# A two-block transformer in fp32r on one core: latent heads in pairs, convolution taps by a table, split weights in halves, other banks, output units among the odd attention's last steps

## What is computed

```python
def even_mixer(h, w_in, q_norm_a, k_norm_a, q_lora_norm, kv_lora_norm, w_uq, w_uk, w_uv, w_out, ...):
    qa, ka, va, ga, cq, ckv, kr, gb = jnp.split(h @ w_in, splits, axis=-1)
    ...
    oa = dense_gqa_attention(qa, ka, va) * jax.nn.silu(ga)
    cq, ckv = rms_norm_2(cq, q_lora_norm), rms_norm_2(ckv, kv_lora_norm)
    qb = (cq @ w_uq).reshape(b, s, B_HEADS, B_NOPE + B_ROPE)
    q_nope, q_rope = qb[..., :B_NOPE], qb[..., B_NOPE:]
    q_rope, k_rope = apply_rope(q_rope, ...), apply_rope(kr, ...)
    q_lat = jnp.einsum('bshd,chd->bshc', q_nope, w_uk)
    ob = mla_attention(q_lat, q_rope, ckv, k_rope, w_uv) * jax.nn.silu(gb)
    return jnp.concatenate([oa, ob], axis=-1) @ w_out

def odd_mixer(h, w_in, sink, w_out, slopes):
    qc, kc, vc, gc = jnp.split(h @ w_in, ...)
    oc = windowed_sink_attention(qc, kc, vc, sink, slopes)      # 16 heads, window 128
    return (oc * jax.nn.silu(gc)) @ w_out
```

## Time and profile before

| | |
|---|---|
| median of 3 executions | 1345.56 us |
| lowest, highest | 1342.73, 1348.53 us |
| profiled execution, its own time | 1347.7 us |
| span of its trace | 1345.9 us |
| TensorE matmul busy | 1308.7 us, 97% |
| VectorE busy | 824.9 us, 61% |
| ScalarE busy | 441.8 us, 33% |
| GpSimd busy | 682.8 us, 51% |
| mean granted TensorE clock | 0.986 |

### The profile page before, as it was taken

The page is one execution under the profiler, slowest core; times in us unless marked ns, Lnnn a source line. Parts: engine busy times, 40 slices in busy tenths (PEclk is TensorE's granted clock), DMA queues, the critical chain, the costliest instruction groups (busy, mean ns, idle before and its releaser), DMA issues.

```text
span 1345.9 us, 19639 instructions
## 1 busy us (share of the span) xinstructions
PE 1308.7 (97%) x7126; PEld 1031.0 (77%) x7126; DVE 824.9 (61%) x1586; ACT 441.8 (33%) x943; POOL 682.8 (51%) x627
## 2 busy tenths in 40 slices
PE   7999999999999999999999999999999999999996
PEld 5898776788888888888888888877566888866575
DVE  4798689933554777777775258654775354055633
ACT  5201455523111212221111243245766223145511
POOL 5864222235676666666677555643000285656650
PEclk9999899999999999999999989999999999999997
DMA  5622101112353455555553224211000122311111
GB/s 178 237 74 78 32 33 33 32 61 81 94 172 96 170 188 190 198 199 195 188 188 101 71 85 142 79 63 48 1 1 1 63 84 84 100 36 48 32 48 63
DMA packets 37524, 130.22 MB, mean 97 GB/s; under 512 B 4544, under 2 KB 4928, under 8 KB 37184
## 3 DMA queue, kind: packets, MB, share of 16 engines
q1 hardware_dynamic: 26640, 93.07, 21.9%
q10 hardware_dynamic: 10800, 35.98, 7.2%
HBM read 126.94 MB, written 2.10 MB: 96 GB/s over the span
## 4 chain that ended last, share of the span: by engine, by line
issue 46%; POOL 36%; PE 16%; DVE 1%; POOLq 1%; ACT 0%; DVEq 0%; ACTq 0%
POOL wlo L1054 21%; PE bank L467 12%; POOL whi L1051 12%; POOL whi L1050 3%; PE bank L980 1%; PE bank L1010 1%; PE bank L990 1%; POOLq L1053 0%; DVE arena L2350 0%; PE bank L538 0%; DVE xbuf L2154 0%; POOL arena L1088 0%; PE bank L555 0%; PE bank L484 0%; POOL wlo L1079 0%
## 5 line engine op out<-in xcount | busy, mean ns | idle before, releaser
L1054 POOL TENSOR_TENSOR wlo<-raw,whi 128x1024 fp32r<-128x1024 f32 x163 | 400.4, 2456 | 13.6
L1050 POOL TENSOR_TENSOR whi<-raw,ones 128x2 fp32r<-128x2 f32 x163 | 42.9, 263 | 571.5 <-DMA raw<-in_w 571.3
L467 PE MATMUL bank<-ysplit,whi 128*128 128x512 f32 x984 | 313.3, 397 | 0.9 <-POOL wlo L1054 0.9
L467 PE MATMUL bank<-hhi,whi 128*128 128x512 f32 x536 | 219.4, 409 | 0.4 <-DVE arena L2217 0.4
L467 PEld LDWEIGHTS bank<-ysplit,whi 128*128 128x128 f32 x984 | 183.6, 189 | 37.6 <-POOL wlo L1054 1.3
L467 PE MATMUL bank<-hhi,wlo 128*128 128x512 f32 x536 | 210.9, 393 | 0.0
L467 PE MATMUL bank<-hlo,whi 128*128 128x512 f32 x536 | 210.5, 393 | 0.0
L467 PE MATMUL bank<-ysplit,wlo 128*128 128x512 f32 x496 | 194.2, 392 | 0.0
L1051 POOL TENSOR_SCALAR whi<-raw 128x1022 fp32r<-128x1022 f32 x163 | 178.1, 1092 | 0.0
L467 PEld LDWEIGHTS bank<-hhi,whi 128*128 128x128 f32 x536 | 101.6, 189 | 25.7 <-issue 6.6
L467 PEld LDWEIGHTS bank<-hhi,wlo 128*128 128x128 f32 x536 | 101.6, 190 | 22.4
(11 more groups left out here) (313 smaller groups left out, 2183.4 us busy)
## 6 DMA issues: line engine op xcount, KB each, us to landing
raw<-in_w SPq DMA_DIRECT2D x171, 512.0 KB, 3.6
arena<-in_ada ACTq DMA_DIRECT2D x48, 512.0 KB, 4.3
xbuf<-in_xT ACTq DMA_DIRECT2D x12, 256.0 KB, 5.3
xbuf<-in_w ACTq DMA_DIRECT2D x1, 2048.0 KB, 10.1
first<-in_w ACTq DMA_DIRECT2D x1, 2048.0 KB, 8.6
out_t<-xbuf SPq DMA_DIRECT2D x8, 256.0 KB, 2.1
xbuf<-in_xT SPq DMA_DIRECT2D x4, 256.0 KB, 6.6
first<-in_uq ACTq DMA_DIRECT2D x1, 768.0 KB, 8.3
```

The costliest lines, as they stand in the source:

```text
L467: m = mm(b[:, :], w[:, s, k * P:(k + 1) * P], x, start=(k == 0 and part == 0), stop=(k == DC - 1 and part == 2))
L1050: g.tensor_tensor(whi[:, s, 0:2], raw[:, s, 0:2], ones[:, :], ALU.mult)
L1054: g.tensor_tensor(wlo[:, s, :], raw[:, s, :], whi[:, s, :].bitcast(F32), ALU.subtract)\
```

## The change

What it does, part by part:

1. **Taps by a table.** `TAPS_AT` gives the number of taps after each step of N: 21 instead of 12 in steps 0 to 11, 50 instead of 66 in steps 12 to 31, 4 in steps 32 and 33, and 3 behind the loop's step 34.
2. **The compressed softmax in PSUM.** `cmp_max` adds, takes the maximum and subtracts in the score bank, and only the last product goes to SBUF. The bank is given back after it.
3. **Low parts in halves.** `low_half` replaces the one 128x1024 operation by two of 128x512.
4. **Biases.** The third bias of e and of o goes to bank 4 (`BIAS_BANK`), and no longer waits for bank 3.
5. **Banks.** `O_BANKS` is (3, 0, 1, 2), equal to `E_BANKS` and `EOUT_REST` and so on their turn; `oq` 3 takes its bank from it and no longer from `TR`. `ekr` takes its bank from `E_BANKS`. `C_FILL` is (3, 0).
6. **Three units' high parts on ScalarE** (`ACT_HIGH`, the last three output units of e).
7. **Latent heads in pairs.** The 64 unrotated rows of two heads make one 128-row product: 4 `key_prep` and 4 `query_prep`, and the rotated rows of four heads one more, twice (`PREP_R`). The rotation of the key moves to steps 1 and 2. All are split in high and low parts (ScalarE `prep_high`, VectorE `prep_low`), and the scores are 3 pairs of 64-row and 3 pairs of 32-row matmuls in fp32r.
8. **The odd attention's end.** `OOUT_FIRST` puts 21 pieces (63 matmuls) of the first three output units in steps 28 to 35, into banks 0, 3 and 7.
9. **The last norm.** The spread is made twice, in two banks. ScalarE copies the second to SBUF, and GpSimd does 3 of the 8 products (`Z_POOL`), for which ScalarE has applied the gain ahead. The stores go in the order `Z_STORE`.

```diff
-PREP_V = (12, 13, 14, 15)
-PREP_K = {12: 0, 13: 1, 14: 2, 15: 3, 20: 4, 21: 5, 24: 6, 25: 7}
-PREP_Q = {12: 0, 13: 1, 16: 2, 17: 3, 20: 4, 21: 5, 24: 6, 25: 7}
+PREP_V = (15, 16, 17, 18)
+PREP_K = {12: 0, 13: 1, 20: 2, 24: 3}
+PREP_Q = {11: 0, 13: 1, 21: 2, 25: 3}
+PREP_R = {10: 0, 19: 1}
+KEY_ROPE = 1
-TAPS_LIGHT = 12
+OOUT_FIRST = {28: ((0, 0, 2),), 29: ((0, 2, 4),), 30: ((0, 4, 6),), 31: ((1, 0, 3),), 32: ((1, 3, 6),), 33: ((2, 0, 3),),
+              34: ((2, 3, 6), (0, 6, 7)), 35: ((1, 6, 7), (2, 6, 7))}
+OOUT_BANKS, OOUT_REST = (0, 3, 7), (1, 2, 0, 3)
+Z_POOL = (0, 1, 2)
+TAPS_AT = (1, 1, 1, 1, 4, 1, 3, 1, 2, 1, 3, 2, 3, 3, 3, 2, 3, 2, 3, 1, 3, 2, 3, 2, 3, 3, 3, 1, 3, 2, 3, 2, 2, 2)
...
-RAW_BANKS, BIAS_BANK = (0, 1, 2), (3,)
+RAW_BANKS, BIAS_BANK = (0, 1, 2), ((3,), (4,))
-O_BANKS = (3, 0, 1, 2, 3, 0, 1, 2)
+O_BANKS = (3, 0, 1, 2)
+ACT_HIGH = (("eout", 5), ("eout", 6), ("eout", 7))
...
-                    for half in range(2):
-                        x = p % 2 * 2 + half
-                        m = mm(banks[half][:, :], QF[x][0:96, qt * P:(qt + 1) * P], KF[x][0:96, :], start=True, stop=True)
+                    j = p - 4
+                    for part, (x, y) in enumerate(((0, 0), (1, 0), (0, 1))):
+                        for half in range(2):
+                            rows = slice(64 * half, 64 * half + 64)
+                            mm(banks[half][:, :], QN[j % 2][x][rows, qt * P:(qt + 1) * P], KN[j % 2][y][rows, :],
+                               start=(part == 0), stop=False)
+                    for part, (x, y) in enumerate(((0, 0), (1, 0), (0, 1))):
+                        for half in range(2):
+                            rows = slice(64 * half + 32 * (j % 2), 64 * half + 32 * (j % 2) + 32)
+                            m = mm(banks[half][:, :], QR[j // 2][x][rows, qt * P:(qt + 1) * P], KR[y][rows, :],
+                                   start=False, stop=(part == 2))
...
-            def key_prep(h):
-                b = bank.take(pe, AB_FILL_BANK if h in (2, 3) else C_R, ("KF", h))
-                mm(b[0:64, :], uk[:, h * HD:(h + 1) * HD], eckv[:, :], start=True, stop=True)\
-                    .then_inc(*pe_did.up(("KF", h)))
+            def key_prep(j):
+                b = bank.take(pe, C_R, ("KN", j))
+                mm(b[:, :], uk[:, j * P:(j + 1) * P], eckv[:, :], start=True, stop=True).then_inc(*pe_did.up(("KN", j)))
...
                 unit("oq", i, first=(lambda k: dve_did.at(("o", "h", k))) if i == len(RAW_O) else None,
-                     pool=TR if i == len(RAW_O) else O_BANKS)
+                     pool=O_BANKS)
...
+                for j, k0, k1 in OOUT_FIRST.get(i, ()):
+                    if k0 == 0:
+                        oout[j] = unit("oout", j, src=y_parts, first=lambda k: dve_did.at(("oy", k)), inline=False,
+                                       pool=OOUT_BANKS)
+                    for k in range(k0, k1):
+                        oout[j](k)
...
+            def low_half(s, half):
+
+                at = slice(half * D // 2, (half + 1) * D // 2)
+                return g.tensor_tensor(wlo[:, s, at], raw[:, s, at], whi[:, s, at].bitcast(F32), ALU.subtract)
...
-                g.tensor_tensor(wlo[:, s, :], raw[:, s, :], whi[:, s, :].bitcast(F32), ALU.subtract)\
-                    .then_inc(w_split.sem, 1)
+                low_half(s, 0)
+                low_half(s, 1).then_inc(w_split.sem, 1)
...
+            pool.wait_ge(*act_did.at(("z", "rsb")))
+            for c in Z_POOL:
+                g.tensor_tensor(xT[:, c, :], xT[:, c, :], rsb, ALU.mult).then_inc(*pool_did.up(("res", c)))
...
-                link(V.tensor_tensor(c3, c3, nmax[:, x:x + 8].unsqueeze(2).to_broadcast([P, HEADS, NCP]), ALU.subtract))
-                V.tensor_tensor(c3, c3, col("slope8", 0, HEADS).unsqueeze(2).to_broadcast([P, HEADS, NCP]), ALU.mult)\
+                link(V.tensor_tensor(S, S, nmax[:, x:x + 8].unsqueeze(2).to_broadcast([P, HEADS, NCP]), ALU.subtract))
...
+                V.tensor_tensor(c3, S, col("slope8", 0, HEADS).unsqueeze(2).to_broadcast([P, HEADS, NCP]), ALU.mult)\
...
-                if i < n:
-                    taps(1 if i < TAPS_LIGHT else -(-len(steps) // (n - i)))
+                if i <= len(TAPS_AT):
+                    taps(TAPS_AT[i] if i < len(TAPS_AT) else len(steps))
```

More of the change, by code:

```diff
@@ L480, in bias @@
                 if k == 0:
-                    bank.take(pe, BIAS_BANK, (tag, "bias", j))
-                b = bank.tiles[BIAS_BANK[0]]
+                    bank.take(pe, BIAS_BANK[j // 2], (tag, "bias", j))
+                b = bank.tiles[BIAS_BANK[j // 2][0]]
                 for w in (whi, wlo):
@@ L548, in sums_once, with spread @@
                     m.then_inc(*pe_did.up((name, "sum")))
-            def spread(name, c0, pool=TR, at=0):
+            def spread(name, c0, pool=TR, at=0, key="spread"):
                 pe.wait_ge(*dve_did.at((name, "stat")))
-                b = bank.take(pe, pool, (name, "spread"))
+                b = bank.take(pe, pool, (name, key))
                 for tt in range(TT):
@@ L556, in spread @@
                            ident[:, :], start=True, stop=True)
-                m.then_inc(*pe_did.up((name, "spread")))
+                m.then_inc(*pe_did.up((name, key)))
             def norm(name, c0=0):
@@ L828, in _ @@
             raw_units("e", 0, RAW_E, raw_e, double_sums, lambda: spread("e", 0, at=TT))
-            unit("ekr", 0, first=lambda k: dve_did.at(("e", "h", k)), pool=TR)
+            unit("ekr", 0, first=lambda k: dve_did.at(("e", "h", k)), pool=E_BANKS)
             spread("f", 0)
@@ L1028, in _ @@
                     c_values(i - 3)
-            for i in range(DC):
-                unit("oout", i, src=y_parts, first=(lambda k: dve_did.at(("oy", k))) if i == 0 else None)
+                for j, k0, k1 in OOUT_FIRST.get(i, ()):
[4 more added lines that the diff above has]
+                        oout[j](k)
+            for j in range(len(oout)):
+                oout[j](DC - 1)
+            for i in range(len(oout), DC):
+                unit("oout", i, src=y_parts, pool=OOUT_REST)
             sums_once("z")
             spread("z", 0)
+            spread("z", 0, key="spread2")
         @block.gpsimd
@@ L1076, in split_part @@
                     return
[L1077 removed]
                 pool.wait_ge(w_hi.sem, u + 1)
[L1079 removed]
+                m = low_half(s, part - 1)
                 if part == 2:
@@ L1095, in c_sink @@
                     .then_inc(*pool_did.up(("C", "sink", i)))
+            splits(0, UNIT[ACT_HIGH[0]])
+            for unit_ in ACT_HIGH:
+                u = UNIT[unit_]
+                pool.wait_ge(w_hi.sem, u + 1)
+                low_half(u % WS, 0)
+                low_half(u % WS, 1).then_inc(w_split.sem, 1)
             end = UNIT[("og", 0)] + WS
-            splits(0, end)
+            splits(UNIT[ACT_HIGH[-1]] + 1, end)
             pool.wait_ge(*dve_did.at("nsink"))
@@ L1603, in _ @@
                 square("z", i, xT[:, i, :], dve_did.at(("x4", i)))
+                if i in Z_POOL:
+                    act.wait_ge(*sq_ready.at(("z", i)))
+                    A(xT[:, i, :], xT[:, i, :], ACT.Copy, scale=col("fn", i)).then_inc(*act_did.up(("z", "gain", i)))
             root("z")
+            act.wait_ge(*pe_did.at(("z", "spread2")))
+            A(rsb, bank.of(("z", "spread2"))[:, :], ACT.Copy).then_inc(*act_did.up(("z", "rsb")))
         @block.vector
@@ L2152, in norm_in_place @@
                 dve.wait_ge(*pe_did.at((name, "spread")))
-                for c in range(DC):
+                for c in range(len(Z_POOL), DC):
                     V.scalar_tensor_tensor(xT[:, c, :], xT[:, c, :], gain(c), bank.of((name, "spread"))[:, :],
@@ L2249, in ab_max, with rope_part, prep_low @@
                         .then_inc(*sm_ready.up(("AB", s)))
[L2251 to L2261 removed]
+            def rope_part(x, part, key):
+                if part == 0:
+                    link(V.stream_shuffle(ropet, x, [(j + 16) % 32 for j in range(32)]))
+                    link(V.tensor_tensor(ropet, ropet, sinT, ALU.mult))
+                else:
+                    link(V.tensor_tensor(x, x, cosT, ALU.mult))
+                    V.tensor_tensor(x, x, ropet, ALU.add).then_inc(*dve_did.up(key))
+            def prep_low(name, j, to):
+                dve.wait_ge(*act_did.at((name, j)))
+                V.tensor_tensor(to[j % 2][1], bank.of((name, j))[:, :], to[j % 2][0].bitcast(F32), ALU.subtract)\
+                    .then_inc(*dve_did.up((name, j)))
+                bank.freed((name, j), dve_did, (name, j))
             def ab_out(p):
@@ L2507 @@
     cosT, sinT = np.cos(angT), np.sin(angT) * sign
+    uq = a["b_w_uq_2"][0].reshape(2, P, HEADS, 96)
+    rope_heads = [[4 * j + 2 * (g % 2) + g // 2 for g in range(4)] for j in range(2)]
+    uq = np.stack([uq[:, :, 2 * j:2 * j + 2, 0:HD].reshape(2, P, P) for j in range(4)]
```

(1 more changed line is left out.)

112 lines of the change are left out of this document (73 added, 39 removed).

## The result

The changed kernel takes 1349.88 us (median of 20 executions, 1342.86 to 1351.12), the kernel before 1345.55 (20 executions in the same rounds). The ratio is 1.0034, 95% interval 1.0019 to 1.0048: slower by a third of a percent, where 1333 and a gain of 0.9% were forecast. Both had a granted clock of 0.986, where 14 of the 20 executions of the changed kernel had 0.984 or less; so the two spans are equal, although the medians differ by 4.3 us.

The account below looks back on a forecast made before the run. TensorE, its matmuls busy 97% of the span, was taken as the bound. The terms summed to −13.8 us: 1333.9 from the profiled 1347.7, 1331.8 against the median; 1333 was given, range 1322 to 1341.

Parts of the forecast that it names:

- Third bias: Bias matmuls of e and o: two waits of 1.1 us go, as bank 4 has nothing to wait for; −0.8.
- `oq` 3: In o, TensorE waits for `oq` 2's bank, +5.0 us; a possible clock fall behind it, bounds 0 and 5.1, +2.5.
- N and the fall at 147: In N, five waits on VectorE's maxima go, −5.9 us, and the half-clock stretch behind 147 us goes, −4.9.
- the allowance of 1.0: In N, 1.0 us of the 6.9 of waits was allowed to stay or come anew.
- both causes go: In N, the SBUF subtraction beside GpSimd (1.87 us wait) and the late taps (5.0 us of waits) both go.
- Halves: Low parts as two operations of 1.29 instead of one of 2.46, hidden under TensorE except in the first few units; +0.2 us.
- Latent heads: In AB: fewer query and key products −7.2 us, scores −2.1, waits for VectorE's low parts +1.8.
- the slower rival: Latent scores: 32-row matmuls run one by one, +19 us over 16 steps instead of −2.1, total 1354; chance 0.03.
- The bound of 0.30 a pair: Latent scores: a 32-row pair costs 0.23 up to 0.30 us; at 0.30 a step takes 1.90, +1.3 in all.
- First unit of o: Start of o: the 0.9 us wait for bank 0, held by e's last output unit, goes; −0.9.
- End of the odd attention: Last eight steps: moved output matmuls fill waits, −3.0 us, with +0.8 for changes of width; −2.2.
- Tail: Last norm: second spread, its copy and GpSimd's three products end slightly later than VectorE before; +0.7 us, bounds −1.5 and +1.5.

Follow-up runs that it names:

- e7: The kernel before with only the third bias of each layer moved to bank 4: 1367.10 us, ratio 1.0157.
- e1: The changed kernel with e's third bias back in bank 3, o's left in bank 4: 1342.03 us, ratio 0.9978 to the kernel before.
- e2: The changed kernel with `oq` 3 back in banks 4 and 5 and o's own tuple of eight: 1345.59 us, ratio 1.0000 to the kernel before.
- e5: The changed kernel with e's third bias in bank 5 and `oq` 3 taken from o's own tuple of eight: 1329.44 us, ratio 0.9871 to the kernel before.
- e6: The kernel before with only `oq` 3 and o's other units taking banks from the tuple shared with e: 1350.17 us, ratio 1.0053.
- e8: The kernel before with only the edits in N, taps by table and compressed softmax in PSUM, low parts whole: 1336.74 us, ratio 0.9940.
- e10: e5 without output units among the odd attention's last steps (`OOUT_FIRST` taken out): 1333.01 us, ratio 0.9917 to the kernel before.
- e3: The changed kernel with e's third bias back in bank 3 and the bank edits of `oq` 3 and o undone: 1338.59 us, ratio 0.9958 to the kernel before.
- e4: As e3, but with e's third bias in bank 5: 1335.11 us, ratio 0.9933 to the kernel before.

## Why the prediction was wrong

**Third bias: −0.8 forecast, +9.5 found.** This is the step that failed. "Bank 4 has nothing to wait for" was not followed in the order of TensorE: bank 4 is one of the pair that the spreads use, and the spread of the same norm is issued inside the second raw unit, just ahead. Its readers are eight products of VectorE, of 0.75 us each with others as long between them. The wait could be worked out from the trace of before: there VectorE's last such product (L1676) begins at 813.7 and ends at 814.5, and the third bias is at its turn at 806.1, 8.4 us earlier. e7 finds the wait in both layers. The prediction did this very analysis for `oq` 3 and not for the bias. Measured: 8.44 of wait for 0.77 saved, and 1.9 through the clock, in all 9.5; e1, which undoes this edit alone, has none of it.

**`oq` 3: +5.0 and +2.5 forecast, +7.9 found** in the profiled execution: 5.49 of wait, and the clock at half for 6.8 us, of which 4.7 lie behind the wait and cost 2.4. The wait is right, and e2, e5 and e6 confirm it as this edit's. That the fall cost 2.4 is luck: 2.5 was the middle between a full fall and none, and no row told them apart.

**N and the fall at 147: −10.8 forecast, −13.4 found** (−10.7 in e8). Right. The sum was low by the allowance of 1.0 that was not needed, and by 1.7 for the fall near 294, which that execution did not have. One reading was incomplete: "both causes go" holds for the softmax in PSUM only together with the halves, since the collision with GpSimd moves on to the tap. The term *Halves* books them as a cost, +0.2; the 1.0 that goes with them is in no term. They do cost GpSimd more than was read (two of 1.38 against one of 2.46), but TensorE doesn't see it: from the end of N to the end of the feed-forward part every unit of the changed kernel ends 13.40 us earlier.

**Latent heads: −7.5 forecast, −2.8 found.** Right in sign, wrong in three sizes. The rows of the changed kernel, to the earlier trace rows:

```profile
979.89 1.98 PE L940 MATMUL bank<-arena,first 128*128 128x512 f32 x4
981.80 0.96 PE L886 MATMUL bank<-hhi,hlo 64*128 64x512 f32 x6
982.70 0.97 PE L891 MATMUL bank<-ysplit,hlo 32*128 32x512 f32 x6
983.60 1.09 PE L900 MATMUL bank<-ident,arena 128*128 128x128 f32 x8
984.53 1.02 PE L935 MATMUL bank<-arena,first 128*128 128x512 f32 x2
985.49 1.09 PE L913 MATMUL bank<-arena,h_first 128*64 128x128 f32 x16
```

- Three pairs of 32 rows take 0.90 (982.70 to 983.60), just as three of 64 rows: a step takes 1.80, not 1.69, and nothing is gained on 1.82 (16 steps: forecast −2.1, found 0). They do run side by side, since six of 0.23 one after another would take 1.4; the slower rival was wrong. The bound of 0.30 a pair was in the text, and the lower end was chosen without a row.
- A query product takes 1.91 (979.89 to 981.80) at 128 columns against 1.79 at 96: the width does cost a little here. Six of them against eight give −2.9 for −3.6.
- Key products were the worst: over AB, summed from each matmul's start to the next one's, key products and the values they stand among took 38.7 us before and take 37.0 now, −1.7 for −3.6. Before, a key product seems to have run partly beside the values. The kernel before shows records that overlap at another step, the two passes of one product (L915) and values (L891); the ends of such records are modelled, so this cause is likely and not shown:

```profile
987.16 0.64 PE L915 MATMUL bank<-arena,first 128*64 128x512 f32 x1
987.18 0.43 PE L891 MATMUL bank<-arena,h_first 128*64 128x128 f32 x2
987.64 0.59 PE L915 MATMUL bank<-arena,first 128*64 128x512 f32 x1
```

- The waits for VectorE were forecast at 1.4 and 0.4 and are 1.30 and 0.37; a third, 0.5, stands at the first latent scores.

**First unit of o: −0.9 forecast, −1.15 found** between the units around it. **End of the odd attention: −2.2 forecast, −2.05 found** between e5 and e10; in the changed kernel's profile only 0.4 is seen, since a fall of 3.4 us lies there. Two errors cancel in that number: the prediction took 3.0 us of waits and gave 0.8 back for changes of width. In fact the wait of 1.1 stays, and what goes is 2.06 (three waits on GpSimd, 1.91, and one of 0.15 on the maxima, all between 1273 and 1284 in the kernel before); for the 0.8 nothing is left over. **Tail: +0.7 forecast, about +1.4 found** between traces that can be compared, near the upper bound. In the changed kernel's profile it is +0.1, because the clock of the kernel before fell earlier in its tail.

Put together, for the two profiled executions: the sum was −13.8, measured was +0.2. The bank that was not followed is 10.3 us off its term, the latent heads 4.7, the end of the odd attention 1.8 (the fall there), `oq` 3 0.4; N gave 2.6 more than forecast, the first unit 0.3, the tail 0.6. That is 13.7 of the 14.0. The other 2.9 of the 17 us between 1333 and the median are the 2.0 by which the changed kernel's profiled execution lies under its median, and the 0.9 by which 1333 lay under the sum.

The bias alone doesn't make the difference to a clear gain. Without its 10.3 us the median would be near 1339.6 (an estimate; no run has this kernel with nothing else altered), inside the range but short of the 1338.8 that counts as faster. e5_banks comes out at 1329.4, but that is not the forecast come true: it is also without the wait of `oq` 3, for which the forecast had +7.5, and would have had to be near 1325.5.

## What to carry to other kernels

A move to a "free" bank must be followed through the whole order: who took it last, how many readers it has, when the last of them runs. Banks handed out in turn couple places that look independent: one unit taken from a pair turned every later user of it, and both bank edits had another price in the changed kernel than alone. A wait inside a matmul stream of an engine that is 97% busy costs its full length, and through the clock an amount that its length doesn't give. The same wait of 2.50 at `ekr` cost 2.6 us in the trace of e3 and 5.5 in that of e1; 2.56 at `oq` 3 cost 4.3 to 5.4 (e2, e3, e4); 8.44 at the bias cost 10.3; and the fall of 10.2 us behind the 1.87 at 145 us cost 4.6 more.
